# Two transformer blocks on one Trainium2 core: norms, state recurrence, gated heads, attention and the sparse mixer rearranged

## The reference

```python
def rmsnorm(x, g):
    y = x * lax.rsqrt(jnp.mean(x * x, axis=-1, keepdims=True) + EPS)
    return y * g

# ssd_scan: 16 heads in 4 groups, chunks of 128 tokens, state 64 x 128 per head, both directions
acum = jnp.cumsum(la, axis=2)                                  # log decays, summed along a chunk
seg = acum[:, :, :, None] - acum[:, :, None, :]
decay = jnp.exp(jnp.where(causal, seg, -jnp.inf))
y_diag = einsum("bclsg,bclsgr,bcsgrp->bclgrp", cb, decay, xdt)
y_off = einsum("bclgn,bcgrpn,bclgr->bclgrp", cc, s_in, jnp.exp(acum))

# hgrn2_gates: lb comes from a softmax over two rows of 1024
f = lb + (1.0 - lb) * jax.nn.sigmoid(f_raw)                    # 2 x 1024 columns of the input product
# hgrn2_readout: norm over each head's 128 columns
o = rmsnorm(o, norm_g) * jax.nn.silu(g)

# attention: 16 heads in 4 groups here, 8 heads in the latent attention
p = exp(s - max(s)) / sum(exp(s - max(s)));  o = p @ v

# nsa_mixer: q (1024), k_c, v_c, k_s, v_s, k_w, v_w (256 each), 48 gates
q, k_s, k_w = rope(q), rope(k_s), rope(k_w);  gates = sigmoid(g)
def compress(t, pos_emb, w1, w2):                              # 15 windows of 32 tokens, 4 groups of 64
    flat = (t[:, cmp_idx] + pos_emb).reshape(B, n_cmp, G, 32 * 64)
    return silu(flat @ w1) @ w2
```

## Time and profile before

| | us |
|---|---|
| median of 3 runs (3274.99 to 3278.75) | 3277.69 |
| the profiled execution, its own time | 3279.47 |
| its span in the trace | 3277.6 |
| TensorE busy | 2748.1 (84%) |
| VectorE busy | 1734.1 (53%) |
| ScalarE busy | 1286.9 (39%) |
| GpSimd busy | 219.6 (7%) |
| mean granted clock of TensorE | 0.91 |

### The profile page before, as it was taken

How to read it: one execution, slowest core, us unless ns; L and a number is a source line. 1 busy time by engine, 2 the same in 40 slices (tenths; PEclk the granted TensorE clock), 3 DMA queues, 4 the chain that set the end, 5 groups by cost and what they waited for, 6 DMA issues and landing times. The chain is left out here.

```text
span 3277.6 us, 36203 instructions
## 1 busy us (share of the span) xinstructions
PE 2748.1 (84%) x13596; PEld 2085.7 (64%) x13596; DVE 1734.1 (53%) x2558; ACT 1286.9 (39%) x1940; POOL 219.6 (7%) x184
## 2 busy tenths in 40 slices
PE   4999867777999967978489969986599899786898
PEld 1766556556888847867433328874478787665786
DVE  2599767536999955356500015524555554136554
ACT  2223244335888844333211115411344443105443
POOL 1000024001011000014000000001000000000000
PEclk7999988887999988989799989997799999869999
DMA  5455400117997143210379964531045454310452
GB/s 224 180 219 217 180 1 1 52 66 261 413 414 300 59 148 116 103 52 1 139 299 411 411 225 180 193 129 52 29 166 193 154 193 167 134 52 1 154 190 74
DMA packets 94348, 536.76 MB, mean 164 GB/s; under 512 B 10848, under 2 KB 12256, under 8 KB 70624
## 3 DMA queue, kind: packets, MB, share of 16 engines
q1 hardware_dynamic: 87120, 508.41, 40.6%
q0 software_dynamic: 6768, 24.64, 2.1%
q10 hardware_dynamic: 288, 1.39, 0.1%
HBM read 599.94 MB, written 22.54 MB: 190 GB/s over the span
## 5 line engine op out<-in xcount | busy, mean ns | idle before, releaser
L1089 PE MATMUL ps<-w_hi,x_hi 128*128 128x512 f32 x1136 | 455.9, 401 | 13.7 <-DVE w_lo L2586 8.2
L1091 PE MATMUL ps<-w_hi,x_lo 128*128 128x512 f32 x1136 | 448.1, 394 | 0.0
L1090 PE MATMUL ps<-w_lo,x_hi 128*128 128x512 f32 x1136 | 447.7, 394 | 0.0
L1089 PEld LDWEIGHTS ps<-w_hi,x_hi 128*128 128x128 f32 x1136 | 217.4, 191 | 59.1 <-DVE w_lo L2586 8.9
L1089 PE MATMUL ps<-x_hi,w_hi 128*128 128x512 f32 (+1 forms) x512 | 204.6, 400 | 56.6 <-DVE x_lo L442 35.4
L1091 PEld LDWEIGHTS ps<-w_hi,x_lo 128*128 128x128 f32 x1136 | 216.5, 191 | 47.1
L1090 PEld LDWEIGHTS ps<-w_lo,x_hi 128*128 128x128 f32 x1136 | 217.6, 192 | 43.6
L1089 PE MATMUL ps<-w_hi,hidden_hi 128*128 128x512 f32 x536 | 210.8, 393 | 7.8 <-DVE hidden_lo L2753 6.0
L1091 PE MATMUL ps<-w_hi,hidden_lo 128*128 128x512 f32 x536 | 209.1, 390 | 0.0
L1090 PE MATMUL ps<-w_lo,hidden_hi 128*128 128x512 f32 x536 | 208.7, 389 | 0.0
L1090 PE MATMUL ps<-x_lo,w_hi 128*128 128x512 f32 (+1 forms) x512 | 197.8, 386 | 0.0
(11 more groups left out here) (623 smaller groups left out, 5645.6 us busy)
## 6 DMA issues: line engine op xcount, KB each, us to landing
weights_A<-in_moe_gate SPq DMA_DIRECT2D x132, 512.0 KB
weights_B<-in_moe_up SPq DMA_DIRECT2D x132, 512.0 KB
weights_A<-in_ffn_gu SPq DMA_DIRECT2D x24, 2048.0 KB, 7.7
weights_B<-in_ffn_gu SPq DMA_DIRECT2D x20, 2048.0 KB, 7.5
weights_C<-in_moe_down SPq DMA_DIRECT2D x66, 512.0 KB
weights_D<-in_moe_down SPq DMA_DIRECT2D x66, 512.0 KB
weights_C<-in_ffn_down SPq DMA_DIRECT2D x24, 1024.0 KB, 6.5
second_weights<-in_moe_gate SPq DMA_DIRECT2D x44, 512.0 KB
```

What stands on the lines that cost most here:

```text
L1089: nc.tensor.matmul(out, w_hi, x_hi, start=first, stop=False)
L1090: nc.tensor.matmul(out, w_hi, x_lo, start=False, stop=False)
L1091: return nc.tensor.matmul(out, w_lo, x_hi, start=False, stop=last)
```

## The change

1. `rms_norm`: squares of even chunks on ScalarE, of odd ones on VectorE, into four buffers. The sums use 32 columns of ones and go to row group 32j of bank 0 (chunk k to j = k mod 4). ScalarE copies the four partial sums, products with 2 columns of ones turn them into one number per token (a token per partition), root and reciprocal are taken of that small tile, VectorE spreads it on a diagonal, and TensorE makes the full tile in bank 2, which the scaling reads.
2. `ssd`: the stage ahead also makes the cumulated decays turned (`AT`, each of 4 row quarters has them) by 32 products of 32 columns. The broadcast is now four products of 32 rows each, one in each row quarter, into banks 0 to 3, single-buffered. The subtraction moves from VectorE into ScalarE's floor (four operations with a bias). The output products go pair by pair over the column halves.
3. `odd_in`: the panels come in the order of `HG_ORDER`, decays first; the gate bounds stand between the pieces, their reciprocal in quarters.
4. `head_norm_gate`: the same steps as in 1, in a stage of its own.
5. `attention`: three buffers in turn for `probs`, diagonals, maxima and sums; waits for the unit three before.
6. `sparse_mixer`: one stage `sparse_in` with split products in 10 half panels of 256 columns; sine tables, rotation, windows and gates run beside them. `compress` takes the window values as the loaded operand (64 columns) and moves 128 weight columns.
7. The constant `pair_sum` (ones where row mod 32 is the column) grows from 16 to 32 columns.

```diff
 rms_norm
-                        nc.scalar.activation(sq[:, k % 2, :], src(k, slice(0, tokens)), ACT.Square)
-                    nc.scalar.activation(root[:], ps[:, 0, 0:tokens], ACT.Sqrt, bias=self.eps[:, 0:1],
+                        nc.scalar.activation(sq[:, k % groups, :], src(k, slice(0, tokens)), ACT.Square)
+                    nc.scalar.activation(parts[0:rows, :], ps[0:rows, 0, 0:tokens], ACT.Copy).then_inc(s["copied"], 1)
+                    nc.scalar.activation(rstd[:], ps[:, 1, 0:2 * nt], ACT.Sqrt, bias=self.eps[:, 0:1],
-                        nc.tensor.matmul(ps[:, 0, 0:tokens], self.c("ones"), sq[:, k % 2, :],
+                        nc.tensor.matmul(ps[32 * j:32 * j + 32, 0, 0:tokens], self.c("ones", 32), sq[:, j, :],
+                    for t in range(nt):
+                        last = nc.tensor.matmul(ps[:, 1, 2 * t:2 * t + 2], parts[0:rows, t * P:(t + 1) * P], self.c("ones", 2, p=rows),
+                    for t in range(nt):
+                        last = nc.tensor.matmul(ps[:, 2, t * P:(t + 1) * P], self.c("ones"), diag[:, t, :], start=True, stop=True)
+                        nc.vector.tensor_tensor(sq[:, k % groups, :], x, x, ALU.mult).then_inc(s["dve_squared"], 1)
-                    nc.vector.reciprocal(rstd[:], root[:]).then_inc(s["inverted"], 1)
+                    nc.vector.reciprocal(rstd[:], rstd[:]).then_inc(s["inverted"], 1)
+                    nc.vector.tensor_tensor(diag[:], self.c("ident").unsqueeze(1).to_broadcast([P, nt, P]),
...
 ssd, broadcast
-                        if u >= 2:
-                            pe.wait_ge(s["diff_done"], u - 1)
-                            pe.wait_ge(s["ea_done"], u - 1)
+                        if u >= 1:
+                            pe.wait_ge(s["ea_done"], u)
-                            last = nc.tensor.matmul(ps[:, b, h * P:(h + 1) * P], LA[:, t, col:col + 1].to_broadcast([P, P]),
-                                                    self.c(("upper", "lower")[d]), start=True, stop=True)
+                            pick = self.c("pair_sum", 32)[rows, col:col + 1].to_broadcast([32, P])
+                            last = nc.tensor.matmul(ps[:, h, 0:P], pick, AT[rows, t * P:(t + 1) * P], start=True, stop=True)
 ssd, output products
+                        for pair in range(2):
+                            for x, decay in ((xdt, E),) if first else ((xdt, E), (S, EA)):
+                                for h in (2 * pair, 2 * pair + 1):
 ssd, ScalarE
-                        nc.scalar.activation(E[:, u % 2, :], E[:, u % 2, :], ACT.Relu).then_inc(s["relu_done"], 1)
+                        for h in range(4):
+                            last = nc.scalar.activation(E[:, u % 2, h * P:(h + 1) * P], ps[:, h, 0:P], ACT.Relu, scale=-1.0,
+                                                        bias=acum[:, t, col:col + 1])
...
+    HG_ORDER = (6, 7, 8, 9, 4, 5, 0, 1, 2, 3)
+                        if p in (2, 3):
+                            bounds(p - 2)
+                        elif 6 <= p < 13:
+                            bounds(p - 4)
+                        if 1 <= n <= 4 and k >= 4:
...
+                            decay(n - 1, k - 4)
...
 attention
-            PR = self.sb(ctx, "probs", [P, 2, 2, nb, SEQ])
+            PR = self.sb(ctx, "probs", [P, 3, 2, nb, SEQ])
-                        if u >= 2:
-                            dve.wait_ge(s["transposed"], u - 1)
+                        if u >= 3:
+                            dve.wait_ge(s["transposed"], u - 2)
...
 sparse_in, TensorE
+                        for u in range(2):
+                            if j < 8:
+                                last = self.product(out, hi[:, cols], lo[:, cols], xh[:, k, :], xl[:, k, :], k == 0, k == KD - 1)
+                            else:
+                                last = self.product(out, xh[:, k, cols], xl[:, k, cols], hi, lo, k == 0, k == KD - 1)
+                        if k == KD - 1 and 1 <= j < 7:
+                            swap(j - 1)
 compress, TensorE
+                            last = nc.tensor.matmul(ps[64 * kv:64 * kv + 64, 0, 0:P], CM[:, kv, h, r, :], W1[:, kv, pos * P:(pos + 1) * P],
```

More of the change, by code:

```diff
@@ L174, in plan @@
         moe(0)
-        for i in range(5):
-            q["A"].append(d["hg_in"][2 * i])
-            q["B"].append(d["hg_in"][2 * i + 1])
+        for n, i in enumerate(self.HG_ORDER):
+            q["AB"[n % 2]].append(d["hg_in"][i])
         q["A"].append(d["hg_out"][0])
@@ L325, in _ @@
+                    last.then_inc(s["spread"], 1)
                 @block.vector
                 def _(dve):
+                    for k in range(1, chunks, 2):
+                        if k >= groups:
+                            dve.wait_ge(s["summed"], k - groups + 1)
+                        x = src(k, slice(0, tokens))
+                        nc.vector.tensor_tensor(sq[:, k % groups, :], x, x, ALU.mult).then_inc(s["dve_squared"], 1)
                     dve.wait_ge(s["rooted"], 1)
-                    nc.vector.reciprocal(rstd[:], root[:]).then_inc(s["inverted"], 1)
+                    nc.vector.reciprocal(rstd[:], rstd[:]).then_inc(s["inverted"], 1)
@@ L829, in ssd @@
             Y = self.sb(ctx, "y", [P, KD, TT])
-            with stage(nc, "transposed copied act_copied sums acum_done diff_done exp_done w_done yinit") as (block, s):
+            AT = self.sb(ctx, "acum_turned", [P, TT])
+            with ExitStack() as early, stage(nc, "transposed copied act_copied sums apart turned_sums turned_copied acum_done diff_done exp_done w_done yinit") as (block, s):
+                apart = self.sb(early, "log_decay_apart", [P, 2, NT, 32])
                 @block.tensor
@@ L913, in outputs @@
                         d, t = steps[i]
[L914 removed]
+                        yb, sb_ = out_bank(u), 7
                         first = i % 4 == 0
@@ L1009, in _ @@
                         weight(u)
-                        if u + 1 < len(units):
-                            diff(u + 1)
                         add_y(u)
@@ L1019, in _ @@
                     for u in range(len(units)):
-                        b = banks(u)[0]
+                        i, g = units[u]
+                        d, t = steps[i]
                         act.wait_ge(s["bcast_done"], u + 1)
@@ L2390, in head_norm_gate @@
         with ExitStack() as ctx:
-            sq = self.sb(ctx, "head_squares", [P, pairs, 2, SEQ])
-            root = self.sb(ctx, "head_root", [P, pairs, 2, SEQ])
-            with stage(nc, "squared summed rooted inverted scaled gated") as (block, s):
+            sq = self.sb(ctx, "head_squares", [P, pairs, 2 * SEQ])
+            diag = self.sb(ctx, "head_rstd_diagonal", [P, pairs, 4, P])
+            rstd = self.sb(ctx, "head_rstd", [P, 4 * pairs, 2])
+            with stage(nc, "squared totals rooted inverted diag_made spread scaled gated") as (block, s):
                 @block.scalar
```

625 lines of the change are left out of this document (387 added, 238 removed).

## The result

| | median, us | runs | ratio to before, 95% interval |
|---|---|---|---|
| before | 3278.22 | 4, 3274.99 to 3279.21 | |
| changed | 3169.31 | 4, 3165.3 to 3178.25 | 0.9673, 0.9651 to 0.9695 |

A forecast was written before the change was run, and what follows sets the result against it. Bounds were taken stage by stage: TensorE where full, otherwise chains of waits between engines. Gains of 17, 10, 23.7, 9, 23.6 and 45 us sum to 128.3, giving a 3149 us median, range 3128 to 3173.

The forecast's parts named there:

- State recurrence: Loop over units: shorter broadcast and VectorE's subtraction gone recover waits for ScalarE's exponential; gain 10 us, bounds -5 and 22.
- rival C: State recurrence gains nothing: its loop of weighting, products, addition and state takes 3.37 us regardless; 3159 us, chance 0.12.
- Rival F: Both input stages: tiny products and shared pieces keep TensorE at 1.2 GHz, doubling 244 us; 3393 us, chance 0.01.
- rival D: Recurrence's output products: column halves really run at once, 11 us more gain; 3138 us, chance 0.08.
- Norms: Norms' fronts: narrower sums and small reciprocals replace the full-width reciprocal; gain 17 us, bounds -12 and 24.
- rival E: Norms: 32-column products take as long as 128-column ones, 29 us off their sum; 3178 us, chance 0.05.
- Gated mixer's input: TensorE's holes at this stage's start and end go; gain 23.7 us, bounds 20 and 26.
- Head norms: Gated heads' norm: a small diagonal replaces the 3.35 us reciprocal per pair; gain 9 us, bounds 4 and 14.
- Attentions: Both attentions: a third buffer removes masking's wait for the transposition two units back; gain 23.6 us, bounds 0 and 26.
- Rival B: Attention keeps its pace because ScalarE's copy or TensorE's product order replaces the freed wait; 3173 us, chance 0.07.
- Last mixer: Input and compression: split products with tables, rotation and windows beside them; 136 us become 91, gain 45, bounds 36 and 52.
- Rival G: Whole kernel: every step comes out at its good bound; 3125 us, chance 0.05.

The follow-up runs named there:

- e5: Changed kernel plus 12 unread 128-row products in TensorE's pause at the start of each recurrence step: 3147.78 us.
- e10: Changed kernel with the whole state recurrence as before, plus the same 12 unread 128-row products per step as e5: 3147.38 us.
- e3: Changed kernel with the recurrence's output products head by head again (decay, then state): 3170.20 us.
- e8: Changed kernel with both attentions on two buffers in turn, as before: 3200.36 us.
- e11: As e5, but the 12 unread products per step have 32 rows instead of 128: 3179.75 us.

## Why the prediction was right, and where not

The time fell into the range, near its end: one term failed by 30 us and the rest came out 11 better than forecast. That it stayed inside was in part luck. The attentions gave 7 us more than forecast, stages of which nothing was forecast gave 8.8, and the other terms fell short by 5. Without the 8.8 it would have been 3178 us, outside the range.

**State recurrence: the failed step.** "I take 10 of the 17.6 us" was wrong in two ways. First, an idle time before one instruction isn't lost time when the next instruction waits as well. I had seen that the subtraction of an inner unit lies in the wait for the products, and then counted its own wait in the other 15 places as gain. Most of it lay in the same wait: near the full clock the addition behind it waits 39.6 us in e5 for 13.3 in e10. These two give 1.7 us for the change, so rival C described the loop; its 3159 us left the clock out. Second, the step counted a shorter broadcast as a gain or as nothing. What it did was to leave TensorE less loaded between its pauses, with 32 rows for 128 and 0.50 us for 1.05; the clock came back later, and a unit at the low level took 4.75 us for 3.43. e5 puts the price at 29.6 us, against 8.4 before the change (e10). The first weightings of two steps, 456.22 and 475.77, are 19.6 us apart, where 16.5 were forecast. Rival F named this mechanism, but I placed it in the input stages, where the clock was 0.98 and 0.96, and priced it only there. The bound of -5 left it out. That the row for the old loop said 0.87, not 1.00, was the sign: a stage at both levels can lose by less work on TensorE, as this one did.

**Product order:** nothing, as taken (e3: 3170.2 against 3169.3), and not the 11 us of rival D.

**Norms:** fronts of 10.94 and 8.51 us for 10.1 forecast, against 14.90 and 12.30; the 256-token one 6.82 for 6.2. By stages the three norms at the low clock gained 4.0, 3.1 and 3.2 us, for 4.8 each. The 32-column products of the first front and of the one at the full clock:

```profile
45.73 4.91 PE L327 MATMUL ps<-squares,constants 128*32 128x512 f32 x16 [7.63 <-ACT squares L309]
...
717.38 3.56 PE L327 MATMUL ps<-squares,constants 128*32 128x512 f32 x16 [2.33 <-ACT squares L309]
```

Before they were 9.98 and 7.52 us, and 3.5 was taken; rival E falls. The latents' norms lost 1.7 us for the 2.2 expected.

**Gated mixer's input:** 181.9 us for 183.5, TensorE busy 178.8 of it at clock 0.98. Both holes are gone. (The terms of the forecast, 176, 2, 3.5 and 1.7, add up to 183.2.)

**Head norms:** 17.2 and 10.9 us for 17.4 and 10.5.

**Attentions:** mechanism right, size low. The saving was 30.6 us instead of 23.6: 7.8 of it in the first attention, where I had priced three pairs at 1.54, and 22.8 for the 19 in the last. What made the savings larger than priced, no run shows. Rival B falls with e8.

**Last mixer:** 82.2 us for 74, and compression 10.3 for 17, at a clock of 1.00 where the old one had 0.50 and the forecast took a value between. (10 x 48 x 0.119 is 57.1, not 57.6.) What stops TensorE in the input, by the view of waits:

```profile
PE ps L1119 <- DVE w_pieces L3509: 7.2, 4, 2.9
PE ps L1119 <- DVE cmp_windows L3547: 4.7, 2, 2.5
```

One of the four is the sine: ScalarE's table load and VectorE's wait for the sines, in whose queue the weight pieces stand, in the timelines of these engines:

```profile
2775.18 1.28 ACT L3495 ACT_TABLE_LOAD   x1
...
2776.99 0.69 DVE L3559 TENSOR_TENSOR rotated<-ps,sin 128x512 f32<-128x512 f32 x1 [2.66 <-ACT sin L3495]
```

TensorE's own busy time, 71.3 us, is also above the 67.6 that I summed.

**The other stages** came out 8.8 us shorter (2.9 of it in the experts of the first block's second half). Nothing in them was changed. They took 2481.1 us before, which lies within the 2472.4 to 2484.2 of the twelve profiles with the change, so the 8.8 us can't be told from what these stages vary by. What makes them vary stays open.

**Rival G**, every step at its good bound, was put at 3125; the good bounds as written add up to 164 us and give 3113. It lies outside the range either way.

## What to carry to other kernels

Before making TensorE's work in a chain of waits smaller, read the granted clock of that stretch: where it stands between the levels, less work on TensorE between pauses can cost more than it saves, and unread full-row products in a pause can pay (e5: 29.6 us of loop, 21.5 of the median). Before crediting the idle time of an instruction that goes, ask whether the next one on that engine would have waited through it. A third buffer is worth its space where the trace shows a write waiting for a reader two units back and no engine is full.

## What the runs showed of the hardware

- The same 12 float32 products of 128 columns in a pause, with 128 or with 32 rows, took the same 2.9 us and left the granted clock of the loop at 0.97 or 0.69 (e5, e11); with none it was 0.64.
- Eight products of 128 rows, 32 output columns and 512 moving columns, in turn over four column groups, took 3.56 us from first to last at a granted clock of 1.00; with 128 output columns they took 7.52 us at 1.00. In float32, 64-column products in two column halves gained nothing by standing next to each other (e3).
- VectorE's weighting of 128x512 took 0.68 us inside a step and 1.57 us at the start of seven of the eight steps, before and after. In the starts at 511.44 (before) and 456.22 (changed) GpSimd's products run beside it; no run tests whether they are the cause.
